# Products of a triangle inverse: 64x64 quarters on the array's diagonal instead of zero-padded copies

## What is computed

```
sa = einsum('zbhvk,zbhk->zbhv', S, -kk_t)
S = S * w_t[..., None, :] + sa[..., :, None] * (kk_t * a_t)[..., None, :] + v_t[..., :, None] * k_t[..., None, :]
o = einsum('zbhvk,zbhk->zbhv', S, r_t)
```

## Time and profile before

| | |
|---|---|
| three runs | 3672.71 us (median), 3660.39 to 3678.71 |
| span of the profiled execution | 3668.3 us (its time as a run is not listed beside it) |
| TensorE busy | 3137.7 us, 86% of the span |
| VectorE, ScalarE, GpSimd busy | 1812.7, 1056.2, 890.9 us |
| scan | from about 1050 to 2198 us of the span |
| mean granted TensorE clock | 0.918 of full speed |

### The profile page before, as it was taken

How to read it: one execution, slowest core, us unless ns; L and a number is a source line. 1 busy time by engine, 2 the same in 40 slices (tenths; PEclk the granted TensorE clock), 3 DMA queues, 4 the chain that set the end, 5 groups by cost and what they waited for, 6 DMA issues and landing times. The chain is left out here.

```text
span 3668.3 us, 73646 instructions
## 1 busy us (share of the span) xinstructions
PE 3137.7 (86%) x30327; PEld 2662.9 (73%) x30327; DVE 1812.7 (49%) x3080; ACT 1056.2 (29%) x1765; POOL 890.9 (24%) x572
## 2 busy tenths in 40 slices
PE   2799779999968988888888973969999994999996
PEld 1688665555547777777777772759999994999995
DVE  5243463344445777776777754752233334333324
ACT  2111102233324545444445531122121212212121
POOL 3111140000032222222222202633232313233222
PEclk9999895699968999999999986979999996999998
DMA  4121210000010000000000004442212204222210
GB/s 144 50 73 52 84 63 21 12 12 11 9 47 20 26 27 31 27 26 26 27 28 29 14 14 136 142 153 77 69 57 69 69 0 158 61 69 59 66 46 34
DMA packets 179998, 196.13 MB, mean 53 GB/s; under 512 B 13067, under 2 KB 140427, under 8 KB 179723
## 3 DMA queue, kind: packets, MB, share of 16 engines
q1 hardware_dynamic: 179756, 192.58, 16.8%
HBM read 148.59 MB, written 43.96 MB: 52 GB/s over the span
## 5 line engine op out<-in xcount | busy, mean ns | idle before, releaser
L2144 POOL TENSOR_TENSOR ff_w_lo<-ff_w,ff_w_hi 128x1024 fp32r<-128x1024 f32 x132 | 313.5, 2401 | 755.6 <-ACT ff_w_hi L2171 565.9
L2304 PE MATMUL ff_gu<-ff_x_hi,ff_w_hi 128*128 128x384 f32 x1408 | 472.5, 336 | 2.8 <-DVE ff_x_lo L2224 2.8
L2304 PE MATMUL ff_gu<-ff_x_lo,ff_w_hi 128*128 128x384 f32 x1408 | 472.0, 335 | 0.0
L2304 PE MATMUL ff_gu<-ff_x_hi,ff_w_lo 128*128 128x384 f32 x1408 | 472.0, 335 | 0.0
L2235 DVE SCALAR_TENSOR_TENSOR ff_th<-ff_th,ff_gu 128x384 f32<-128x384 f32 x88 | 48.8, 554 | 582.1 <-ACT ff_th L2184 582.1
L1390 ACT ACTIVATE sc_XTd<-sc_XT 64x512 f32<-64x512 f32 x300 | 188.1, 627 | 358.5 <-DVE sc_XT L1487 353.8
L2304 PEld LDWEIGHTS ff_gu<-ff_x_hi,ff_w_hi 128*128 128x128 f32 x1408 | 265.6, 189 | 4.4 <-DVE ff_x_lo L2224 3.6
L2304 PEld LDWEIGHTS ff_gu<-ff_x_hi,ff_w_lo 128*128 128x128 f32 x1408 | 265.6, 189 | 0.8
L2304 PEld LDWEIGHTS ff_gu<-ff_x_lo,ff_w_hi 128*128 128x128 f32 x1408 | 265.4, 189 | 0.0
L2249 DVE TENSOR_TENSOR ff_y<-ff_dn,ff_y 128x512 f32<-128x512 f32 x264 | 180.4, 690 | 136.4 <-PE ff_dn L2317 136.2
L2317 PE MATMUL ff_dn<-ff_w_hi,ff_a_lo 128*128 128x512 f32 x528 | 205.8, 390 | 0.0
(11 more groups left out here) (275 smaller groups left out, 6698.7 us busy)
## 6 DMA issues: line engine op xcount, KB each, us to landing
ff_w<-in_w_ffn_in SPq DMA_DIRECT2D x88, 512.0 KB, 5.1
ff_w<-in_w_ffn_out SPq DMA_DIRECT2D x44, 512.0 KB, 3.6
sc_rk<-scratch_rkv SPq DMA_DIRECT2D x24, 512.0 KB, 3.3
scratch_rkv<-co_tm SPq DMA_DIRECT2D x12, 768.0 KB, 3.9
pj_x<-in_x SPq DMA_DIRECT2D x13, 512.0 KB, 3.6
co_w<-in_w_in SPq DMA_DIRECT2D x13, 512.0 KB, 4.6
scratch_scan<-sc_out SPq DMA_DIRECT2D x24, 260.0 KB, 2.5
mo_sc<-scratch_scan SPq DMA_DIRECT2D x24, 260.0 KB, 2.9
```

Of the source, the lines that this page charges most:

```text
L2144: nc.gpsimd.tensor_tensor(w_lo[:, q, x, :], w[:, q, x, :], w_hi[:, q, x, :].bitcast(F32), ALU.subtract).then_inc(done, 1)
L2304: last = nc.tensor.matmul(gu[:, g, m, 0:GRP], ww[:, q, m, k * P:(k + 1) * P], xx[:, k, g * GRP:(g + 1) * GRP], start=(j == 0), stop=(j == ...
```

## The change

The products `x` and `t` read XT and Y themselves as left operand, with 64 rows and 64 columns of chunk c: the quarter (c, c) of the array. `y` reads the same 64x64 block of AT. The right operand is also only the chunk's 64 rows. The copies into YD are gone; one copy of XT into XTd is left, unpadded, after level 5, for the solve. The waits for `bd` before products go, and the other waits of a product become holds. XTd is not zeroed any more.

```diff
@@ -1085,7 +1085,7 @@
         ET = sb("sc_ET", [P, 2, 2, RH, P])
         FT = sb("sc_FT", [P, 2, 2, RH, P])
         YD = sb("sc_YD", [P, 2, RH, P])
-        XTd = sb("sc_XTd", [P, 2, 2, RH, P])
+        XTd = sb("sc_XTd", [P, 2, 2, RW])
         Y = sb("sc_Y", [P, 2, RW])
         X = sb("sc_X", [P, 2, RW])
         XT = sb("sc_XT", [P, 2, RW])
@@ -1170,7 +1170,7 @@
                 eng.wait_ge(in_loaded[st.s], 16 * 3 * (st.g + 1))
 
 
-        PER_FRONT_BD = 2 * LEVELS - 1
+        PER_FRONT_BD = 1
 
         def order(c, s):
 
@@ -1283,7 +1283,7 @@
                 for part in (AT[:, :, :, :], YD[:, :, :, :], H[:, :, :, :], H_meta[:, :, :]):
                     nc.gpsimd.memset(part, 0.0)
                 for p in range(2):
-                    for t in (ET, FT, XTd):
+                    for t in (ET, FT):
                         nc.gpsimd.memset(t[:, :, p], 0.0)
                 nc.gpsimd.memset(out[:, :, RW:RW + RH], 0.0).then_inc(zeroed, 1)
                 pool.wait_ge(zeroed, 4)
@@ -1374,21 +1374,10 @@
                             nc.scalar.activation(to.rearrange("p j c t -> p (j c) t"), heads(bank[:, st.bank(slot), :]), ACT.Copy).then_inc(free[s][slot % 3], 1)
                     if name == "dv":
                         copy(D_V, DV[:, s, par, :])
-                    if name == "y" and level:
-                        slot = Y_SLOT[level]
+                    if name == "t" and level == LEVELS - 1:
+                        slot = XT_SLOT[level]
                         act.wait_ge(free[s][slot % 3], st.taken(slot))
-                        for c in range(2):
-                            last = nc.scalar.activation(YD[half(c), s, :, half(c)], heads(Y[half(c), s, :]), ACT.Copy)
-                        last.then_inc(bd[s], 1)
-                    if name == "t":
-                        slot = XT_SLOT[level]
-                        if level:
-                            act.wait_ge(free[s][slot % 3], st.taken(slot))
-                        else:
-                            act.wait_ge(first_xt[s], 3 * st.n + 3)
-                        for c in range(2):
-                            last = nc.scalar.activation(XTd[half(c), s, par, :, half(c)], heads(XT[half(c), s, :]), ACT.Copy)
-                        last.then_inc(bd[s], 1)
+                        nc.scalar.activation(XTd[:, s, par, :], XT[:, s, :], ACT.Copy).then_inc(bd[s], 1)
 
                 def back(st, k):
                     if k not in (0, 3):
@@ -1611,38 +1600,46 @@
                         fill(D_V, last)
 
                     def product(slot, lhsT, rhs):
-                        b = claim(slot)
+                        hold(pe, free[s][slot % 3], st.before(slot), pe_passed)
+                        b = bank[:, st.bank(slot), :]
 
                         for h in range(RH):
                             for c in range(2):
-                                last = nc.tensor.matmul(b[half(c), half(h)], lhsT[:, h, half(c)], rhs(h), start=True, stop=True)
+                                last = nc.tensor.matmul(b[half(c), half(h)], lhsT(h, c), rhs[half(c), half(h) if rhs.shape[1] > CHUNK else slice(0, CHUNK)],
+                                                        start=True, stop=True)
                         fill(slot, last)
 
-                    n = PER_FRONT_BD * st.n
+                    def ready(slot):
+                        hold(pe, free[s][slot % 3], st.taken(slot), pe_passed)
+
+                    A = lambda h, c: AT[half(c), s, h, half(c)]
+                    left = lambda t: lambda h, c: t[half(c), s, half(h)]
                     if name == "y":
 
                         if level == 0:
-                            product(Y_SLOT[0], AT[:, s], lambda h: eye[:, :])
+                            product(Y_SLOT[0], A, eye[:, :])
                         else:
                             if level == 1:
-                                pe.wait_ge(first_x[s], st.n + 1)
+                                hold(pe, first_x[s], st.n + 1, pe_passed)
                             else:
-                                need(X_SLOT[level - 1])
-                            product(Y_SLOT[level], AT[:, s], lambda h: X[:, s, half(h)])
+                                ready(X_SLOT[level - 1])
+                            product(Y_SLOT[level], A, X[:, s, :])
                     if name == "x":
 
-                        need(Y_SLOT[level])
-                        pe.wait_ge(bd[s], n + 2 * level - 1)
-                        product(X_SLOT[level], XTd[:, s, par], lambda h: Y[:, s, half(h)])
+                        ready(Y_SLOT[level])
+                        if level == 1:
+                            hold(pe, first_xt[s], 3 * st.n + 3, pe_passed)
+                        else:
+                            ready(XT_SLOT[level - 1])
+                        product(X_SLOT[level], left(XT), Y[:, s, :])
                     if name == "t" and level:
 
-                        need(Y_SLOT[level])
-                        pe.wait_ge(bd[s], n + 2 * level)
+                        ready(Y_SLOT[level])
                         if level == 1:
-                            pe.wait_ge(first_xt[s], 3 * st.n + 3)
+                            hold(pe, first_xt[s], 3 * st.n + 3, pe_passed)
                         else:
-                            need(XT_SLOT[level - 1])
-                        product(XT_SLOT[level], YD[:, s], lambda h: XT[:, s, half(h)])
+                            ready(XT_SLOT[level - 1])
+                        product(XT_SLOT[level], left(Y), XT[:, s, :])
 
                 def back(st, k):
                     s, g, par = st.s, st.g, st.par
@@ -1659,7 +1656,7 @@
                         pe.wait_ge(rh_ok[s], 2 * g + k // 3 + 1)
                         hold(pe, bd[s], PER_FRONT_BD * (st.n + 1), pe_passed)
                         for h in range(RH):
-                            last = nc.tensor.matmul(b[half(c), half(h)], XTd[half(c), s, par, h, half(c)], U1[half(c), s, half(h)], start=True, stop=True)
+                            last = nc.tensor.matmul(b[half(c), half(h)], XTd[half(c), s, par, half(h)], U1[half(c), s, half(h)], start=True, stop=True)
                     elif k in (2, 5):
                         for j in range(4):
                             cols = slice(j * P, (j + 1) * P)
@@ -1677,7 +1674,7 @@
                     pe.wait_ge(free[0][D_V % 3], Step(0, -1, 0).taken(D_V))
                     for c in range(2):
                         for h in range(RH):
-                            last = nc.tensor.matmul(bank[half(c), 6 + c, half(h)], XTd[half(c), 0, 0, h, half(c)], DV[half(c), 0, 0, half(h)],
+                            last = nc.tensor.matmul(bank[half(c), 6 + c, half(h)], XTd[half(c), 0, 0, half(h)], DV[half(c), 0, 0, half(h)],
                                                     start=True, stop=True)
                         last.then_inc(m_full, 1)
                     for c in range(2):
```

## The result

| | runs | ratio to the kernel before |
|---|---|---|
| kernel before | 3670.34 us (median of 9) | 1 |
| changed kernel | 3690.99 us (median of 9) | 1.0064, 95% interval 1.0046 to 1.0082 |
| changed kernel, once more, in a second series | 3706.69 us (median of 10) | 1.0082, 1.0051 to 1.0113 |

The forecast was 3647 us, faster. The kernel became slower by 0.6 to 0.8%, and both medians lie above the range. One of the nine runs of the changed kernel, 3737.74 us, counts as slow and is left out of the ratio. The profile shown here is of an execution of the second series (3715.46 us; span 3713.7). It is kept beside the profile of before (span 3668.3).

A forecast was written before the change was run, and what follows sets the result against it. Bound by TensorE from the last t to x of level 1, then by VectorE to x of level 3. Terms -20.8 - 2.1 + 3.6 - 3.6 - 0.6 - 2 = -25.5 us; 3668.3 - 25.5 + 4.4 = 3647 us, range 3622 to 3676.

The forecast's parts named there:

- t of level 5: Product right behind dv: its wait for the YD copies goes and the gain passes on whole, -20.8 us, bounds 17 and 24.5.
- changes of form: Switching between 64x64 and other products costs 0.09 us, net once per half-window on TensorE-bound places: -2.1 us, between -4 and +2.
- x products: Of 62.7 us idle before x, nothing is gained without the XTd copies: 0, at most 2.4 us in all.
- what is late next: Without the copies, x at levels 2 and 3 gains nothing: VectorE's H scaling holds the carry, its Y holds x.
- Pace of the products: Each 64x64 product, alternating between diagonal quarters, still takes 0.98 us start to start; bounds 0.89 and 1.96.
- rival of serial quarters: Quarters sharing a PSUM bank run in turn: product 1.96 us, about 3930 us; chance 0.10, partly for a slightly slower product.
- rival of faster products: Products take 0.89 us instead of 0.98, another 15 us gained, so 3632 us; chance 0.10.
- Start and end: No XTd zeroing before the scan's first matmul, -3.6 us; shorter XTd copy before RH in the last half-window, -0.6.
- The holds: 0.05 us more at three tight handovers per half-window (y level 2, x levels 3 and 4): +3.6 us, 0 to +11.
- rival for the holds: Weights cannot load ahead past a hold: seven products per half-window pay 0.14 us, 23.5 for 3.6, so 3667 us; chance 0.10.
- The clock: Three of 25 t products of level 5 run at 1.2 GHz; those falls may go: -2 us, between 0 and -5.
- bad ends: The unknown costs at their worst bounds: 3668.3 - 9 + 4.4 = 3664 us; at good ends 3633.

## Why the prediction was wrong

- **t of level 5 (-20.8): right.** Its wait went whole. With the holds reordered, full-clock pairs in the loop take 40.63 + 41.64 us, 2.3 below before, 28 us in 12 pairs; t and the changes of form were to give 22.9. The changes of form were not measured by themselves.
- **x products (0) and what is late next: right.** 63.8 us of idle time stayed, and the carry took over at level 2.
- **Pace of the products: right**, 0.98 us. The rival of serial quarters is out. The Trainium skill, "TensorEngine Tiling (Array Packing)", Restrictions and Gotchas, has it that different row tiles cannot access the same PSUM bank at once; by that a product would take 1.96 us, and the trace disagrees: two quarters of different rows write one bank in 0.98. The rival of faster products is out as well.
- **Start and end: right.** The first matmul of the scan waits 18.31 us, 3.5 less than in the earlier trace rows (2.6 to 3.5 less in the other profiles without the zeroing); the last solve 0.90 in place of 1.66.
- **The holds (+3.6, at most +11): mis-sized, the first failed step.** I took 0.05 us at three handovers from a solve product which has one hold, and that one last. The products have two or three, the open wait first: 0.31 to 0.50 us. At full clock that costs 13 us more than one hold does. My rival for the holds, a lost weight load of 0.14 us for each of seven products, had another cause: each hold behind the open wait takes its 0.15 us, and their order decides.
- **The clock (-2, at most 0): the wrong sign, and the step that decides.** I asked only whether the falls at t of level 5 would go. Inside the loop they went: two such products took 1.98 us before, none takes over 1.15 now. I did not ask what the longer gap before x of level 3, whose 1.51 us stood in my rows, would do. From 1.5 to 1.9 us it brought some 53 us (1.0082 with the gap, 0.9938 with the same holds and the gap filled, 1.4% of 3670). -25.5, with 13 in place of 3.6 and +53 in place of -2, is +39, where the second series had 32 us and the first 21; the rest is open, and how often the clock falls varies from run to run. No rival joined the two, so none of them ended at 3691. (The bad ends of the terms add up to -8.2, not -9, which moves the range by less than 1 us.)

The text had named a handover of over 0.2 us as what would make it wrong. That is what happened.

## What to carry to other kernels

A wait that is an instruction of its own costs about 0.15 us when it stands behind one that is still open: put the wait that ends last right in front of the instruction, and those that are long over ahead of it. When a change makes TensorE's gaps longer, even by 0.4 us, look at the granted clock behind them before counting the gain. A gap that cannot be closed can be filled with work that is thrown away; here 16 such matmuls were worth 1.4%.

## What was not expected of the hardware

A gap longer by 0.5 us at one place per half-window changed the time by 1.7%, 1.4% of it because TensorE then ran at 1.2 GHz for 3 to 27 us at a time. How often it falls varies between executions of one kernel: the changed kernel's ten runs go from 3677 us (mean clock 0.911) to 3726 (0.896), while the kernel with one hold stays within 13 us. And TensorE's queue works through holds while it waits only if they stand ahead of the open wait: three of them in that order hand over in 0.14 us, the other way round in 0.45 to 0.50.
